# A three-block transformer kernel: the squares of the halved norms are summed on GpSimd, and the query operand is scaled ahead of the last root

## The reference: what is computed

```python
def rmsnorm(x, g):
    return x * lax.rsqrt(jnp.mean(x * x, axis=-1, keepdims=True) + 1e-6) * g

x = x + rmsnorm(f, norm_g[layer, 3])            # the post norm, and the residual
down = rmsnorm(x, kv_norm_g) @ kv_w_down        # a pre norm of the new x ...
c_kv = rmsnorm(down[..., :256], kv_a_norm_g)
h = rmsnorm(x, norm_g[layer + 1, 0])            # ... and another gain on the same x
c_q = rmsnorm(h @ q_w_down, q_norm_g)
```

## Time and profile before

| what | value |
|---|---|
| median of three runs | 2256.86 us |
| the profiled execution's own time | 2257.56 us |
| its span in the trace | 2255.8 us |
| TensorE busy (products) | 2166.7 us, 96% |
| VectorE, ScalarE, GpSimd busy | 1304.3, 918.6, 116.4 us |
| mean granted TensorE clock | 0.981 of full speed |

### The profile page before, as it was taken

The page is one execution under the profiler, slowest core; times in us unless marked ns, Lnnn a source line. Parts: engine busy times, 40 slices in busy tenths (PEclk is TensorE's granted clock), DMA queues, the critical chain, the costliest instruction groups (busy, mean ns, idle before and its releaser), DMA issues.

```text
span 2255.8 us, 38226 instructions
## 1 busy us (share of the span) xinstructions
PE 2166.7 (96%) x15190; PEld 1744.0 (77%) x15190; DVE 1304.3 (58%) x2047; ACT 918.6 (41%) x1533; POOL 116.4 (5%) x136
## 2 busy tenths in 40 slices
PE   6999999988999999899999999999999999999998
PEld 4866666676788888867788888888867887888887
DVE  5856867865654635766637636456755555434345
ACT  4854433434432323546645323234345444322222
POOL 0002222211000000100000000001000000000001
PEclk9999999989999999999989999999999999999999
DMA  4310010014232332211211333323211232323322
GB/s 140 95 44 15 15 28 16 25 40 131 77 101 93 101 93 84 66 44 35 64 58 56 103 98 99 102 86 101 71 47 43 79 112 84 103 93 101 95 87 72
DMA packets 54332, 169.02 MB, mean 75 GB/s; under 512 B 7065, under 2 KB 13465, under 8 KB 54065
## 3 DMA queue, kind: packets, MB, share of 16 engines
q1 hardware_dynamic: 54192, 167.07, 24.0%
HBM read 164.95 MB, written 2.10 MB: 74 GB/s over the span
## 4 chain that ended last, share of the span: by engine, by line
PE 87%; DVE 8%; ACT 3%; issue 2%; DMA 0%; SPq 0%; DVEq 0%; ACTq 0%
PE bank L2120 53%; PE bank L2700 3%; PE bank L2273 2%; PE bank L2308 2%; PE bank L2594 2%; PE bank L2205 2%; PE bank L2325 2%; PE bank L2155 2%; PE bank L2395 1%; PE bank L2613 1%; PE bank L2631 1%; PE bank L2407 1%; PE bank L2222 1%; PE bank L2239 1%; PE bank L2710 1%
## 5 line engine op out<-in xcount | busy, mean ns | idle before, releaser
L1275 DVE TENSOR_TENSOR w_lo<-w_raw,w_hi 128x1024 fp32r<-128x1024 f32 (+4 forms) x313 | 356.2, 1139 | 198.5 <-ACT w_hi L686 193.7
L2120 PE MATMUL bank<-a_hi,w_hi 128*128 128x512 f32 x1168 | 457.0, 391 | 1.8 <-DVE w_lo L1275 1.8
L2120 PE MATMUL bank<-a_lo,w_hi 128*128 128x512 f32 x1168 | 454.5, 389 | 0.0
L2120 PE MATMUL bank<-a_hi,w_lo 128*128 128x512 f32 x1168 | 454.5, 389 | 0.0
L686 ACT ACTIVATE w_hi<-w_raw 128x1024 fp32r<-128x1024 f32 (+4 forms) x313 | 301.4, 967 | 211.4 <-PE bank L2120 196.8
L2120 PEld LDWEIGHTS bank<-a_hi,w_hi 128*128 128x128 f32 x1168 | 219.3, 188 | 49.0 <-issue 2.0
L2120 PEld LDWEIGHTS bank<-a_hi,w_lo 128*128 128x128 f32 x1168 | 219.3, 188 | 46.6 <-issue 1.2
L2120 PEld LDWEIGHTS bank<-a_lo,w_hi 128*128 128x128 f32 x1168 | 219.2, 188 | 45.5
L2120 PE MATMUL bank<-b_hi,w_hi 128*128 128x512 f32 x520 | 202.9, 390 | 4.0 <-DVE down_kv L1836 3.4
L2120 PE MATMUL bank<-b_hi,w_lo 128*128 128x512 f32 x520 | 202.3, 389 | 0.0
L2120 PE MATMUL bank<-b_lo,w_hi 128*128 128x512 f32 x520 | 202.3, 389 | 0.0
(11 more groups left out here) (382 smaller groups left out, 3914.6 us busy)
## 6 DMA issues: line engine op xcount, KB each, us to landing
w_raw<-in_f0gu SPq DMA_DIRECT2D x44, 512.0 KB, 3.5
w_raw<-in_f1gu SPq DMA_DIRECT2D x44, 512.0 KB, 3.5
w_raw<-in_f2gu SPq DMA_DIRECT2D x44, 512.0 KB, 3.5
w_raw<-in_f0dn SPq DMA_DIRECT2D x16, 512.0 KB, 3.5
w_raw<-in_f1dn SPq DMA_DIRECT2D x16, 512.0 KB, 3.6
w_raw<-in_f2dn SPq DMA_DIRECT2D x16, 512.0 KB, 3.5
w_raw<-in_kl SPq DMA_DIRECT2D x12, 512.0 KB, 3.5
w_raw<-in_in SPq DMA_DIRECT2D x10, 512.0 KB, 3.6
```

Of the source, the lines that this page charges most:

```text
L1275: dve.tensor_tensor(lo[:, 0:n, :], raw[r][:, 0:n, :], hi[:, 0:n, :].bitcast(F32), ALU.subtract).then_inc(w_split[r], 1)
L2120: mm = pe.matmul(bank[r][:, :], w[r][:, k, :], a[:, k, :], start=(k == 0 and n == 0), stop=(k == kt - 1 and n == 2))
```

## The change

Four things are done.

1. At the three boundaries the pre norm's squares are added up on GpSimd (`add_x_square`): for each half tile 1 is added to tile 0, then tiles 2 to 7, seven additions of 128x256. TensorE's product with ones is left once a half (`sum_x`): for the first half ahead of tile 2 of the second half, for the second half inside the unit that follows the guest units, ahead of its third tile (`sum_inside`), at the first boundary ahead of tile 3 of the first query unit.
2. ScalarE's square of tile `j` now waits for GpSimd's addition of tile `j-2` (of tile 1 for tiles 2 and 3), where it waited for TensorE's product of tile `j-2`.
3. At the first boundary ScalarE writes the query operand's high part ahead of the second half's root, and VectorE its low part ahead of the second half's reciprocal (`first_queries`, handed in as `aside`).
4. The query units go to banks 3, 4 and 0 (`QD_BANK`) instead of 0, 1 and 2, so that the first two do not wait for `kvd`'s units to be read out; the values' tiles go in the order 2, 1, 3, 0, and the latent norm's products stand ahead of tile 6 of the second query unit instead of ahead of its first.

The core of the diff:

```diff
+SUMS = ON_POOL - SPLIT_FROM + DT - 1
...
+            def add_x_square(b, name, j, h):
+                first = NORM_AT[name][1]
+                at_h = PART[h]
+                pool.wait_ge(*((sq_ready, first + j + 1) if h else half(half_sq, sq_count(b, DT + j))))
+                if j == 1:
+                    pool.wait_ge(*((std_ready, NORM_AT[name][0]) if h else half(half_std, 2 * b + 1)))
+                else:
+                    pool.wait_ge(*((sq_used, SQ_USED_AT[name] + j - 1) if h else half(half_summed, SUMS * b + 1 + j)))
+                before = sq[first % 2] if j == 1 else sq_sum
+                pool.tensor_tensor(sq_sum[:, at_h], before[:, at_h], sq[(first + j) % 2][:, at_h], ALU.add)\
+                    .then_inc(sq_used if h else half_summed, 1)
...
+                        for h in range(2):
+                            for j in range(1, DT):
+                                add_x_square(b, BOUNDS[b][3], j, h)
...
             def square_x(b, name, j, h):
                 if j >= 2:
-                    act.wait_ge(*((sq_used, SQ_USED_AT[name] + j - 1) if h else half(half_sum, (DT + 1) * b + 1 + j - 1)))
+                    used = max(j - 2, 1)
+                    act.wait_ge(*((sq_used, SQ_USED_AT[name] + used) if h else half(half_summed, SUMS * b + 2 + used)))
...
+            def sum_x(b, name, h):
+                pe.wait_ge(*((sq_used, SQ_USED_AT[name] + n - 1) if h else half(half_summed, SUMS * (b + 1))))
+                pe.matmul(bank[6 - h][:, PART[h]], const("ones"), sq_sum[:, PART[h]], start=True, stop=True)\
+                    .then_inc(sum_ready if h else half_sum, 1)
...
                         if (h, k) == (0, 2):
                             sum_part(b, post, 1)
-                        sum_x(b, pre, k, h)
+                        elif (h, k) == (1, 2):
+                            sum_x(b, pre, 0)
...
+            for u in range(3):
+                for k in range(DT):
+                    if (u, k) == (0, 3):
+                        sum_x(0, "n_mla", 1)
+                    elif (u, k) == (1, 6):
+                        norm("n_ckv")
```

More of the change, by code:

```diff
@@ L744, in root_part @@
                 if h == 0:
-                    act.wait_ge(*half(half_sum, (DT + 1) * b + (DT + 1 if before else 1)))
+                    act.wait_ge(*half(half_sum, 2 * b + 1 + int(before)))
                     act.wait_ge(*(half(half_rstd, 2 * b + 1) if before else (rstd_ready, i)))
@@ L814, in token_halves @@
                         root_part(b, pre, 0, True)
+                if aside is not None:
+                    aside()
                 root_part(b, pre, 1, True)
@@ L1765, in _, with first_queries @@
             root("n_f0")
+            def first_queries():
+                for j in range(DT):
+                    if j == 3:
+                        ahead_of(low, FLAT.index(("qd", 1)))
+                    gained_low("q", j)
             def ffn(tag):
@@ L1828, in _, with read_down @@
             ffn("f0")
-            for j in range(2):
-                gained_low("q", j)
             dve.wait_ge(const_loaded, 16 * LOADS)
-            def read_down(name, dst, r):
+            def read_down(name, dst, r, b):
                 dve.wait_ge(unit_done[r], START[name][r] + 1)
-                dve.tensor_tensor(dst[:, r, :], bank[r][:, :], rstd[:, :], ALU.mult).then_inc(bank_free[r], 1)
+                dve.tensor_tensor(dst[:, r, :], bank[b][:, :], rstd[:, :], ALU.mult).then_inc(bank_free[r], 1)
             for r in range(2):
-                read_down("kvd", down_kv, r)
-            for j in range(2, DT):
-                gained_low("q", j)
+                read_down("kvd", down_kv, r, r)
             dve.wait_ge(unit_done[2], START["kvd"][2] + 1)
             dve.tensor_tensor(k_rope[:, :], bank[2][:, :], rstd[:, :], ALU.mult).then_inc(bank_free[2], 1)
-            for u in (1, 2):
-                ahead_of(low, FLAT.index(("qd", 0)) + u)
+            ahead_of(low, FLAT.index(("qd", 2)))
             rope_a, rope_b = gconv, gpad
@@ L2165, in sum_part @@
                     pe.wait_ge(std_ready, i)
[L2166 removed]
+                    pe.wait_ge(*half(half_summed, SUMS * b + 2))
                 else:
@@ L2176, in sum_part, with sum_inside, inside @@
                 mm.then_inc(sum_ready if h else half_sum, 1)
-            def sum_x(b, name, k, h):
-                i, first, n = NORM_AT[name]
-                pe.wait_ge(*((sq_ready, first + k + 1) if h else half(half_sq, sq_count(b, DT + k))))
-                mm = pe.matmul(bank[6 - h][:, PART[h]], const("ones"), sq[(first + k) % 2][:, PART[h]], start=(k == 0),
-                               stop=(k == n - 1))
-                if k < n - 1:
-                    mm.then_inc(sq_used if h else half_sum, 1)
-                else:
-                    mm.then_inc(sum_ready if h else half_sum, 1)
+            def sum_x(b, name, h):
+                n = NORM_AT[name][2]
+                pe.wait_ge(*((sq_used, SQ_USED_AT[name] + n - 1) if h else half(half_summed, SUMS * (b + 1))))
+                pe.matmul(bank[6 - h][:, PART[h]], const("ones"), sq_sum[:, PART[h]], start=True, stop=True)\
+                    .then_inc(sum_ready if h else half_sum, 1)
+            def sum_inside(name, unit):
+                b = next(n for n, row in enumerate(BOUNDS) if row[2] == name)
+                def inside(r, k):
+                    if (r, k) == (unit, 2):
+                        sum_x(b, BOUNDS[b][3], 1)
+                return inside
             def wide_halves(name, operand):
@@ L2554, in _ @@
             dense("kvd", lambda r: opnd["a"], normed("kv"), wide="n_mla", count=GUESTS)
-            dense("qd", lambda r: opnd["b"], normed("q"), lambda i, r: norm("n_ckv") if r == 0 else None)
+            for u in range(3):
+                c = START["qd"][u]
+                pe.wait_ge(w_split[u], c + 1)
+                if u != 1:
+                    pe.wait_ge(bank_free[3 if u == 0 else 0], START["qd"][3 if u == 0 else 0])
+                for k in range(DT):
[3 more added lines that the diff above has]
+                        norm("n_ckv")
+                    pe.wait_ge(normed_low, NORMED_AT["q"][0] + k + 1)
+                    for n, (w, a) in enumerate(((w_hi, opnd["b"][0]), (w_lo, opnd["b"][0]), (w_hi, opnd["b"][1]))):
+                        mm = pe.matmul(bank[QD_BANK[u]][:, :], w[u][:, k, :], a[:, k, :], start=(k == 0 and n == 0),
+                                       stop=(k == DT - 1 and n == 2))
+                mm.then_inc(unit_done[u], 1)
             def values(n):
```

48 lines of the change are left out of this document (27 added, 21 removed).

## The result

The changed kernel takes 2280.5 us, the median of five runs: 2272.88, 2275.27, 2280.5, 2285.13 and 2694.43. The kernel before takes 2256.86 us (five runs, 2252.4 to 2257.79). The run of 2694.43 had a mean clock of 0.748 against 0.972 to 0.977 in the others, and the ratio leaves it out; the median of the other four is 2277.9. The ratio is 1.0109, 95% interval 1.0089 to 1.0128: slower, by 21 to 24 us as one takes the median. The forecast was 2281. The profiled execution took 2285.13 us, span 2283.3.

What follows compares the result with a forecast made beforehand. TensorE was taken to bound the kernel, with VectorE close behind it. 16.8 us in three boundaries, +2.9, +0.6 and -0.7 behind them and +4.5 for the clock make 24.1 us, so 2281 us; range 2264 to 2291.

Steps and rivals of the forecast that it cites:

- Bound: At the boundary TensorE is full, VectorE close behind: its last low part ends 3.6 us ahead of TensorE's end.
- forecast bound 1.7: Most that taking products with ones off TensorE can gain with VectorE unchanged: 1.7 us a boundary.
- VectorE's 0.65: Two VectorE waits at the boundary, 0.47 and 0.18 us, for squares that waited for TensorE, go away.
- Part 2, the ring: First half's root waits behind TensorE's second-half tiles, delaying VectorE's low part 2: 2.05 us a boundary, net +1.4.
- Part 3, the additions: Eleven of GpSimd's 14 additions a boundary each hold VectorE 0.54 us by a port lock: 5.9 us.
- TensorE's end: At the boundary TensorE ends 1.9 us behind VectorE's last low part.
- Part 4: Behind the boundaries: late second-half root costs +2.9 us at the second, +0.6 at the third; first gains, -0.7.
- Part 5, the clock: TensorE's sparse work in the boundary may halve its clock: 1.5 us a boundary, between 0 and 3.4; +4.5.
- Sum: Whole kernel: 16.8 + 2.9 + 0.6 - 0.7 + 4.5 = 24.1 us slower, median 2281 us.

Runs made afterwards that it cites:

- small_adds: The changed kernel with each of GpSimd's boundary additions cut to 2 columns instead of 256, all waits kept: 2259.07 us, ratio 1.001.
- first_root_early: The changed kernel with the first half's product with ones ahead of tile 0 of the second half instead of tile 2: 2266.24 us, ratio 1.0056.
- boundary_filled: The changed kernel with a product of constants on TensorE ahead of each boundary wait for a low part but the first: 2274.96 us, ratio 1.0083.
- queries_only: The kernel before with only the change's query part (query scaling ahead of the last root, other banks and orders): 2248.85 us, ratio 0.9976.

## Why the prediction was right

**Bound.** Right. TensorE was full at the boundary and yet not what could be shortened: without blocking and ring, 17.6 us of products were worth 3 x 2.1 us (forecast bound 1.7 and VectorE's 0.65 a boundary).

**Part 2, the ring.** Forecast 2.05 us of waiting and +1.4 net; 2.03 and +1.6 with the clock up (small_adds). In the changed kernel it's 2.76, as the groups in the ring ran partly at half clock. The prediction added ring and clock as two terms, and they feed each other: the ring's wait makes the idle time that lets the clock fall. first_root_early shows 4 us at the first and third boundary, clock included, for what the term had at 1.4.

**Part 3, the additions.** Forecast eleven hits of 0.54, 5.9 us; measured eleven new ones, 0.48 each in the first boundary, 5.3 us busier, and the last low part 6.0 later than in small_adds (33.6 against 27.6 after the start; the other 0.7 is the longer ring). That it is one waiting for the other was read from two pairs of rows, and holds in all 36 long instructions, 33 of them new, as many as forecast.

**TensorE's end.** 1.9 us behind the last low part; 2.1 in small_adds.

**Part 4.** Second boundary +2.9: measured 2.9 (8.77 us behind the guest units against 5.89). Third +0.6: 0.9, from 11 us behind the guest units on, and 1.9 by the ledger, as the fall of the clock at 1670.8 lasts 10.2 us instead of 6.8. First -0.7: the query norm's first product comes 22.4 us behind the guest units instead of 23.0, -0.6, and by the forecast's own two terms: the latent norm's product 1.0 later (forecast 1.1), the chain from it 1.6 shorter (1.6 to 2.0).

**Part 5, the clock.** Forecast 1.5 a boundary, by a guess between 0 and 3.4; about 2.2, 2.1 and 1.5, by boundary_filled, two falls in each. The mis-sized term is this one, 4.5 for 5.8. The boundary without it is 5.3 us longer than before (forecast 5.6), with it 7.2 in the mean (forecast 7.1). One sign was missed: TensorE was idle for 8.3 us in the boundary, not 10 and more, as its products ran longer at half clock (`bank<-a_lo,g_hi` 327 ns in the mean instead of 281).

**Sum.** In the profiled executions the ledger has 27.5 us for the forecast's 24.1: 21.7 in the boundaries (forecast 21.3), -0.5, 3.2 and 1.9 behind them (-0.7, 2.9, 0.6), and 1.2 ahead of the first, where nothing was changed.

**Left out.** The fall in the attention, up to 7.3 us in an execution, which comes and goes, and whose cause stayed open. It is in the profiled execution of before and in the changed one, so it drops out of the ledger's difference. The forecast was set on the median of before, 2256.86; its runs with a mean clock of 0.985 or more have 2250.5 in the mean, and from there the same 24.1 us would have led to 2274.6. The changed kernel's own runs, the one of 2694.43 aside, go from 2272.88 to 2285.13. So the parts were right within 1.3 us each, but the agreement of 2281 with 2280.5 to half a microsecond is luck.

**Open.** Why the clock fell in the attention in some executions and not in others with the same instructions there. Shown is only that edits ahead of it change how often it falls (a mean clock of 0.985 or more in 14 of 64 runs of before, in 11 of 12 of queries_only), and that filling the waits prevents it. Two additions per square were not tried, so whether the price of part 3 goes on rising with more of them is open too.

## What to carry to other kernels

Before work is moved to GpSimd, look at what VectorE does meanwhile: if its list is dense and its instructions read two SBUF operands, most of GpSimd's additions cost VectorE a wait (0.5 us for 128x256, eleven of fourteen here), and whoever waits for VectorE gets it. Taking work from the engine that bounds the kernel is worth only as much as its feeder is ahead, here 2.1 of 5.9 us a boundary. And before a difference of a few microseconds is put down to an edit, cut the spans into stretches and compare those that the edit does not touch.

## What the runs showed of the hardware

In the attention of the kernel before the clock of TensorE fell to 1.2 GHz although no single wait was longer than 1.9 us (1123.5 to 1126.9: 1.54 us busy of 3.4), and in other executions the same instructions, 1.62 us busy of 3.4, passed at 2.4 GHz. One such fall cost up to 7.3 us, more than most edits here. Products of constants that filled 1.88 and 1.33 us of waiting removed it.

A GpSimd write of 128x256 beside VectorE's instructions with two SBUF operands cost them nothing. An addition of the same size held them until it had ended, and they ended 0.28 or 0.29 us behind it: 0.48 to 0.54 us lost in all but three cases (0.57 us instead of 0.48, where the addition was nearly over). The reciprocals beside it kept their 1.74 us. GpSimd's own addition grew from 0.72 to as much as 0.95 us in the changed kernel.
